# Expert sums issued in pairs, a modulation row made later, and more PSUM banks for the first norm, in a one-core decoder step

## The chip, the cores and the metric

The kernel runs on one core of a Trainium2 chip. The metric is the device time of one execution in microseconds. Everything below is from three timed runs of the kernel before and one profiled execution of it.

## The reference, cut to what matters

One decoder layer over 1088 tokens: 1024 of a prompt and 64 of a sample group (8 sequences of 8). A mixer (a gated short convolution and gated linear attention) comes first, then a PEER layer that picks, for each token and head, 16 of 16384 experts. Both are wrapped in norms with a modulation (shift, scale, gate) made from a condition.

```python
def decoder_layer(x, c, conv_buf, gla_state, params):
    mod = (jax.nn.silu(c) @ w_ada + b_ada)[:, None, :]
    sh1, sc1, g1, sh2, sc2, g2 = jnp.split(mod, N_MOD, axis=-1)
    h = rms_norm(x, n_mix_pre) * (1.0 + sc1) + sh1
    m, new_buf, new_state = mixer(h, ...)
    x = x + g1 * rms_norm(m, n_mix_post)
    h = rms_norm(x, n_ffn_pre) * (1.0 + sc2) + sh2
    x = x + g2 * rms_norm(peer(h, ...), n_ffn_post)
...
def peer(h, wq, subkeys, u_tab, v_tab):
    ...
    gate = jax.nn.softmax(top_v, axis=-1)
    act = jax.nn.gelu(jnp.einsum('thkd,td->thk', u_tab[expert], xb))
    return jnp.einsum('thk,thkd->td', gate * act, v_tab[expert])
```

## The kernel before

**Staging.** The 1088 tokens lie in nine tiles: two of the prompt (128 tokens each), the sample tile (64), six more of the prompt. Three tiles make a block (block 0: tiles 0, 1 and the sample tile). After a conditioning phase and the attention heads, each block goes through `mix_phase`, `merge_phase`, `out_phase`, `norm_phase`, `keys_phase` and `pick_phase`; `last_phase` closes the kernel. The experts that `pick_phase` chooses are fetched and used by `Gather`, which runs token by token beside the phases of the next block, and alone in the last phase. How many tokens each phase takes is fixed by `SHARES` (L2266) through `Turns`: 67, 35, 28, 30, 64 and 72 in block 1's phases, 87, 46, 35, 39, 84 and 93 in block 2's.

**Gather.** For one token the 128 chosen rows (8 heads x 16) are fetched by one indirect DMA from GpSimd (L1042): 128 rows of u and v, 2048 floats each. Ten such buffers exist (`NUV`). TensorE spreads the token's h over 128 partitions in two half spreads of 512 columns (L1059, banks 0 and 1; half spread s waits for dot s - 2). VectorE multiplies each half with u and adds up (L1164), ScalarE makes a gelu of four tokens (L1134), VectorE weighs them (L1184). TensorE then sums gate times v (L1079): each token of a group of four adds a matmul of 32 output rows per half of D, at PSUM partitions j*32 (j is the token's row group: 0 to 3 by turns in a prompt tile, 0 and 1 in the sample tile) in bank 2 or 3. All eight matmuls of a group stand in one block behind half spread 8q + 11 (`spread` and `summed`, L1046 to L1083), and `v_mm`, raised by the last one, frees the four buffers for GpSimd's next fetches. [...]

**Modulation and the first norm.** `Modulation` makes the rows GATE1, SHIFT2, GAIN2 and GATE2 (nine rows each: the prompt's and eight sequences') while block 0 is in its phases, before the gather needs `gat.uv`, whose buffers it borrows. It has eight chunks of 512 columns, at the steps `AT` (L1218): 2 MB of weights by SyncE, eight matmuls into four row groups (L1289), a copy by ScalarE (L1309), a folding matmul (L1299), two operations of VectorE on 9x512 (L1319, L1321), and a save by SyncE. Chunks 6 and 7 (GATE2) come at steps 0 and 2 of block 0's `norm_phase`; their weights are fetched in `merge_phase`. `norm_phase` needs rows spread over all partitions: `spread_row` (L1743) does it with two matmuls of K = 9 into two banks. It has banks 4 to 7 for that, so in block 0 the prompt's and the sample's GATE1 rows come first, GAIN2 takes their banks once VectorE has used them, SHIFT2 takes the banks of GAIN2. VectorE goes through squares (L1838), gate, addition of x and squares (L1843, L1847, L1850), gain (L1856), shift (L1861), each over three tiles, then TensorE transposes (L1780).

## Time and profile before

| | us |
|---|---|
| median of 3 runs | 4248.77 (4247.3 to 4263.02) |
| profiled execution | 4251.55, span 4249.7 |
| TensorE busy | 3195.1 (75%) |
| VectorE busy | 2578.3 (61%) |
| GpSimd busy | 1605.2 (38%) |
| ScalarE busy | 839.7 (20%) |
| DMA | 1348.98 MB, mean 317 GB/s |
| first gather issued | 1040.43 |

In a profile PE is TensorE's matmuls, PEld its weight loads, DVE VectorE, ACT ScalarE, POOL GpSimd, SPq SyncE's queue. [...] Averages over the whole span mix three regimes, so the numbers are to be read by stage.

### The profile page before, as it was taken

What the parts mean: (1) busy time and instruction counts of PE and PEld (TensorE: products, weight loads), DVE (VectorE), ACT (ScalarE), POOL (GpSimd) and SP (SyncE); (2) the same over time, 40 slices, a digit from 0 to 9 for tenths busy, and PEclk for the clock granted to TensorE, in tenths of its full rate; (3) what the DMA queues carried; (4) which work ended last, traced back from release to release, by engine and by line L of the source; (5) the groups of instructions that cost most, each with busy time, mean ns of one, the idle gap of its engine ahead of it and who ended that gap; (6) DMA issues with size and microseconds to landing.
All of it is one profiled execution on the core that took longest, in us unless ns stands there. A gap on an engine that the chain in (4) does not pass through costs nothing. (4 is left out here: it accounts for less than half of the span.)

```text
span 4249.7 us, 46772 instructions
## 1 busy us (share of the span) xinstructions
PE 3195.1 (75%) x15717; PEld 1732.2 (41%) x15717; DVE 2578.3 (61%) x7848; ACT 839.7 (20%) x1341; POOL 1605.2 (38%) x1354
## 2 busy tenths in 40 slices
PE   7999988885688876766788777777666666666676
PEld 5899977754265542521255353243111111111111
DVE  2553453348765656878765566678776555655554
ACT  4233323332123222111124212111101000000000
POOL 2101105423365653443355454343333333333332
PEclk9999988977699887987899898698666666666666
DMA  7011105523899999998999999999999999999998
GB/s 263 32 46 47 52 30 187 211 97 143 316 368 393 378 412 365 367 366 343 354 394 408 391 401 402 378 413 379 360 389 382 411 415 412 407 412 411 412 408 341
DMA packets 219399, 1348.98 MB, mean 317 GB/s; under 512 B 27710, under 2 KB 37246, under 8 KB 76956
## 3 DMA queue, kind: packets, MB, share of 16 engines
q0 software_dynamic: 156672, 1140.92, 66.6%
q1 hardware_dynamic: 62492, 205.06, 13.3%
q8 instruction: 131, 2.15, 0.2%
q14 instruction: 104, 0.85, 0.1%
HBM read 1317.77 MB, written 28.10 MB: 317 GB/s over the span
## 5 line engine op out<-in xcount | busy, mean ns | idle before, releaser
L1164 DVE CUSTOM_DVE_ANT_0 peer_uv<-peer_uv,all_PS 128x512 f32<-128x512 f32 x2176 | 1436.3, 685 | 1042.4 <-DMA peer_uv<-in_uv,peer_idx 520.7
L1042 POOL DMA_INDIRECT peer_uv<-in_uv,peer_idx x1088 | 1056.4, 971 | 1495.4 <-PE all_PS L1079 1176.8
L1059 PE MATMUL all_PS<-peer_hT,peer_sel 96*128 96x512 bf16 x2176 | 982.7, 467 | 845.6 <-DVE peer_halves L1164 801.1
L1059 PEld LDWEIGHTS all_PS<-peer_hT,peer_sel 96*128 96x128 bf16 x2176 | 205.3, 101 | 1659.7 <-DVE peer_halves L1164 1330.9
L1079 PE MATMUL all_PS<-peer_uv,peer_zw 128*32 128x512 f32 x4352 | 817.3, 851 | 2.2 <-DVE peer_zw L1184 2.2
L932 POOL TENSOR_TENSOR flow_w_lo<-flow_w,flow_w_hi 128x1024 fp32r<-128x1024 f32 (+1 forms) x204 | 463.7, 2278 | 566.6 <-ACT flow_w_hi L925 566.1
L1134 ACT ACTIVATE peer_ge<-peer_pre 128x4 f32<-128x4 f32 x272 | 55.9, 205 | 2092.5 <-DVE peer_pre L1170 2092.5
L1079 PEld LDWEIGHTS all_PS<-peer_uv,peer_zw 128*32 128x32 f32 x4352 | 154.1, 141 | 426.9 <-issue 424.4
L952 PE MATMUL all_PS<-mix_h_hi,flow_w_hi 128*128 128x384 f32 (+1 forms) x672 | 283.0, 421 | 35.7 <-POOL flow_w_lo L932 31.9
L925 ACT ACTIVATE flow_w_hi<-flow_w 128x1024 fp32r<-128x1024 f32 (+1 forms) x204 | 203.7, 1003 | 317.4 <-PE all_PS L954 164.9
L953 PE MATMUL all_PS<-early_h_h_low,flow_w_hi 128*128 128x384 f32 (+1 forms) x672 | 225.6, 336 | 0.0
L954 PE MATMUL all_PS<-mix_h_hi,flow_w_lo 128*128 128x384 f32 (+1 forms) x672 | 224.9, 335 | 0.0
L1164 DVE DVE_READ_ACCUMULATOR2_ANT peer_halves<- 128x1 f32 x2176 | 179.7, 83 | 0.0
L952 PE MATMUL all_PS<-turned_h_hi,flow_w_hi 128*128 128x384 f32 (+1 forms) x384 | 177.5, 462 | 1.4 <-PEq L143 1.4
L952 PEld LDWEIGHTS all_PS<-mix_h_hi,flow_w_hi 128*128 128x128 f32 x672 | 134.2, 200 | 75.0 <-issue 40.9
L182 POOL CAST stream_w_hi<-stream_heads_w 128x1024 fp32r<-128x1024 f32 x16 | 16.6, 1038 | 357.7 <-PE all_PS L617 293.3
L953 PEld LDWEIGHTS all_PS<-early_h_h_low,flow_w_hi 128*128 128x128 f32 x672 | 131.6, 196 | 7.7
L953 PE MATMUL all_PS<-turned_h_lo,flow_w_hi 128*128 128x384 f32 (+1 forms) x384 | 131.4, 342 | 0.0
L954 PE MATMUL all_PS<-turned_h_hi,flow_w_lo 128*128 128x384 f32 (+1 forms) x384 | 130.6, 340 | 0.0
L954 PEld LDWEIGHTS all_PS<-mix_h_hi,flow_w_lo 128*128 128x128 f32 x672 | 130.3, 194 | 0.0
L1659 PE MATMUL all_PS<-flow_w_hi,out_x_hi 128*128 128x256 f32 (+1 forms) x288 | 108.6, 377 | 18.5 <-DVE join_gate_low L992 15.8
L952 PEld LDWEIGHTS all_PS<-turned_h_hi,flow_w_hi 128*128 128x128 f32 x384 | 78.7, 205 | 26.3 <-issue 25.9
(310 smaller groups left out, 4763.0 us busy)
## 6 DMA issues: line engine op xcount, KB each, us to landing
flow_w<-in_w_gate_ab SPq DMA_DIRECT2D x48, 512.0 KB, 5.4
flow_w<-in_w_query SPq DMA_DIRECT2D x48, 512.0 KB, 7.0
flow_w<-in_w_conv SPq DMA_DIRECT2D x36, 512.0 KB, 4.3
peer_uv<-in_uv,peer_idx POOLq DMA_INDIRECT x1088, 10.7
cond_w<-in_w_ada SPq DMA_DIRECT2D x6, 2048.0 KB, 10.1
stream_heads_w<-in_w_heads SPq DMA_DIRECT2D x24, 512.0 KB, 4.8
peer_uv<-in_w_ada SPq DMA_DIRECT2D x6, 2048.0 KB, 8.9
flow_w<-in_w_proj_b SPq DMA_DIRECT2D x24, 512.0 KB, 5.7
```

What stands on the lines that cost most here:

```text
L182: nc.gpsimd.tensor_copy(hi, raw).then_inc(high, 1)
L925: nc.scalar.activation(self.hi[:, i % self.pairs, 0:nk], self.raw[:, i % self.raws, 0:nk], ACT.Copy).then_inc(self.high, 1)
L932: nc.gpsimd.tensor_tensor(self.lo[:, i % self.pairs, 0:nk], self.raw[:, i % self.raws, 0:nk], self.hi[:, i % self.pairs, 0:nk].bitcast(F32 ...
L952: nc.tensor.matmul(out, w_hi[:, k, :], x.hi[:, k, :], start=(k == 0), stop=False)
L953: nc.tensor.matmul(out, w_hi[:, k, :], x.lo[:, k, :], start=False, stop=False)
L954: last = nc.tensor.matmul(out, w_lo[:, k, :], x.hi[:, k, :], start=False, stop=(k == nk - 1))
L1042: self.nc.gpsimd.indirect_dma_start(out=self.uv[:, n % self.NUV, :], out_offset=None, in_=self.A["uv"], in_offset=bass.IndirectOffsetOnAxi ...
L1059: nc.tensor.matmul(PS[:, f, :], self.sel[:, m:m + 1].broadcast_to([3 * GR, P]), self.hT[:, g % self.NH, f * 512:(f + 1) * 512], start=True ...
L1079: last = nc.tensor.matmul(PS[j * GR:(j + 1) * GR, 2 + e, :], self.zw[:, z, GR - 1 - c:2 * GR - 1 - c], self.uv[:, n % self.NUV, D + e * 51 ...
L1134: nc.scalar.activation(self.ge[:, q % self.ND, :], self.pre[:, q % self.ND, :], ACT.Gelu_apprx_tanh).then_inc(M["gelled"], 1)
L1164: nc.vector.tensor_tensor_reduce(part, part, PS[:, f, :], 1.0, 0.0, ALU.mult, ALU.add, self.halves[:, d, f, e:e + 1]).then_inc(M["dotted"], 1)
L1659: nc.tensor.matmul(bank(j), x.hi[:, k, tok], w_hi, start=(k == 0), stop=False)
```

## The change

Three parts.

1. `summed` is called four times per group, for two tokens and one half of D each, behind four half spreads in a row (8q + 10 to 8q + 13) rather than twice behind 8q + 11.
2. The two chunks of GATE2 leave `Modulation`. A new class `LastGate` makes the row in block 0's `pick_phase`, in four rounds of 256 columns at steps 4, 9, 14 and 19, with buffers and semaphores of its own.
3. In block 0's `norm_phase` the row spreadings use banks 0 to 3 as well (the gather has not begun): both GAIN2 rows are spread at the start, SHIFT2's prompt row once all gates are used, SHIFT2's sample row once the prompt gains are.

```diff
-            if n >= BT and f == 1 and n % BT == 1:
-                for e in range(2):
-                    self.summed(pe, n // BT - 1, e)
+            q, p = divmod(s - 2 * BT - 2, 2 * BT)
+            if q >= 0 and p < 4:
+                self.summed(pe, q, p)
...
-    def summed(self, pe, q, e):
+    def summed(self, pe, q, p):
...
-        if e == 0:
+        e, pair = divmod(p, 2)
+        if p == 0:
             pe.wait_ge(M["weighed"], q + 1)
...
-        for n in range(BT * q, BT * q + BT):
+        for n in range(BT * q + 2 * pair, BT * q + 2 * pair + 2):
...
-        if e:
+        if p == 3:
             last.then_inc(M["v_mm"], 1)
...
-    AT = (8, 12, 17, 22, 29, 33, NORM, NORM + 2)
-    LINES = ((GATE1, 0.0), (SHIFT2, 0.0), (GAIN2, 1.0), (GATE2, 0.0))
+    AT = (8, 12, 17, 22, 29, 33)
+    LINES = ((GATE1, 0.0), (SHIFT2, 0.0), (GAIN2, 1.0))
...
+class LastGate:
+    AT = (4, 9, 14, 19)
+    WN = 256
...
+    def fetch(self, sp, s):
+        for r in self.here(s + 3):
+            half = slice(r % 2 * self.WN, (r % 2 + 1) * self.WN)
+            if r:
+                sp.wait_ge(self.used, r)
+            sp.dma_start(self.w[:], self.A["w_ada"][10 + r // 2, :, :, half]).then_inc(self.w_in, 16)
+            if r:
+                sp.wait_ge(self.lined, r)
+            for dst, src in ((self.bias, "ada_rows"), (self.gain, "gain_rows")):
+                sp.dma_start(dst[:, :], self.A[src][6 + r // 2:7 + r // 2, half].broadcast_to([NC, self.WN])).then_inc(self.small_in, 16)
...
+    def product(self, pe, s):
+        CT = P // 4
+        for r in self.here(s):
+            pe.wait_ge(self.w_in, 16 * r + 16)
+            if r:
+                pe.wait_ge(self.rowed, r)
+            for k in range(KD):
+                j = k % 4
+                last = self.nc.tensor.matmul(self.PS[j * CT:(j + 1) * CT, FRONT + 1, 0:self.WN], self.later.cols[:, k, :], self.w[:, k, :],
+                                             start=(k < 4), stop=(k >= 4), skip_group_check=True)
+            last.then_inc(self.used, 1)
+        for r in self.here(s - 1):
+            pe.wait_ge(self.rowed, r + 1)
+            if r:
+                pe.wait_ge(self.added, r)
+            self.nc.tensor.matmul(self.PS[0:NC, FRONT + 2, 0:self.WN], self.later.folds, self.row[:, :],
+                                  start=True, stop=True).then_inc(self.folded, 1)
...
+    def make_line(self, dve, s):
+        for r in self.here(s - 2):
+            dve.wait_ge(self.folded, r + 1)
+            dve.wait_ge(self.small_in, 32 * r + 32)
+            if r:
+                dve.wait_ge(self.kept, 16 * r)
+            self.nc.vector.tensor_tensor(self.line[:, :], self.PS[0:NC, FRONT + 2, 0:self.WN], self.bias[:, :], ALU.add).then_inc(self.added, 1)
+            dve.wait_ge(self.added, r + 1)
+            self.nc.vector.tensor_tensor(self.line[:, :], self.line[:, :], self.gain[:, :], ALU.mult).then_inc(self.lined, 1)
...
+        GATE_AT, GAIN_AT, SHIFT_AT = ((FRONT, FRONT + 2), (0, 2), (FRONT + 2, 0)) if part.samples else ((FRONT,), (FRONT,), (FRONT + 2,))
+        Y_AT = FRONT + 2
+        row = lambda at: PS[:, at:at + 2, :].rearrange("p b d -> p (b d)")
...
-            spread_row(GATE1, 0, False)
+            spread_row(GATE1, GATE_AT[0], False)
             if part.samples:
-                spread_row(GATE1, 1, True)
+                spread_row(GATE1, GATE_AT[1], True)
+                spread_row(GAIN2, GAIN_AT[0], False)
+                spread_row(GAIN2, GAIN_AT[1], True)
             else:
-                spread_row(GATE2, 1, False)
+                spread_row(GATE2, Y_AT, False)
...
                 if stage == 2 and i == 0:
-                    pe.wait_ge(gated, prompts)
-                    spread_row(GAIN2, 0, False)
-                    if part.samples:
-                        pe.wait_ge(gated, nt)
-                        spread_row(GAIN2, 1, True)
-                    else:
+                    pe.wait_ge(gated, nt)
+                    if not part.samples:
+                        spread_row(GAIN2, GAIN_AT[0], False)
                         pe.wait_ge(fin.done, 1)
-                        spread_row(SHIFT2, 1, False)
+                    spread_row(SHIFT2, SHIFT_AT[0], False)
                 if stage == 3:
+                    pe.wait_ge(gained, prompts)
                     if part.samples and i == 0:
-                        pe.wait_ge(gained, nt)
-                        spread_row(SHIFT2, 1, False)
-                    if i == sample:
-                        pe.wait_ge(h2_done, prompts)
-                        spread_row(SHIFT2, 1, True)
-                    pe.wait_ge(gained, prompts)
+                        spread_row(SHIFT2, SHIFT_AT[1], True)
...
             for j in range(NJ):
                 gat.turn(sp, upto(j))
+                if gate:
+                    gate.fetch(sp, j)
+                    gate.keep(sp, j)
```

The rest of `LastGate` is the copy of a product's rows by ScalarE and the save of a line by SyncE, at the next steps; `pick_phase` calls all of them by engine and step.

## Rows read from the trace of the kernel before

**Rows 1.** The page's slices of the span in tenths, 106 us each.
```profile
PEclk9999988977699887987899898698666666666666
DMA  7011105523899999998999999999999999999998
```

**Rows 2.** The chain that ended last, pieces of it: start us, us, what.
```profile
3748.11 12.78 DMA peer_uv<-in_uv,peer_idx
3762.97 3.12 PE all_PS L1079 x16
```

**Rows 3.** Table by stretch: start:end, length, busy (count) by engine, PEclk, DMA share, GB/s.
```profile
1137.00:1347.00 210.00, 189.56 (x1062) 135.14 (x1058) 122.67 (x326) 63.24 (x84) 123.45 (x92) 0.96 0.97 384
1347.00:1565.00 218.00, 169.65 (x969) 113.36 (x969) 127.97 (x328) 44.42 (x69) 119.37 (x89) 0.90 0.97 386
1660.00:1850.00 190.00, 149.61 (x828) 93.70 (x828) 138.99 (x597) 35.05 (x65) 91.72 (x75) 0.94 0.94 371
1850.00:2090.00 240.00, 159.70 (x481) 36.00 (x481) 189.30 (x700) 21.15 (x44) 78.24 (x79) 0.76 0.90 355
2090.00:2357.00 267.00, 224.67 (x1198) 142.27 (x1198) 161.25 (x431) 79.53 (x102) 147.00 (x115) 0.94 0.99 395
2357.00:2612.00 255.00, 191.81 (x1060) 117.81 (x1062) 155.74 (x404) 43.29 (x72) 129.44 (x104) 0.90 0.99 396
2728.00:2950.00 222.00, 174.90 (x930) 101.00 (x930) 162.81 (x674) 33.83 (x68) 101.03 (x88) 0.90 0.97 391
2950.00:3234.00 284.00, 181.64 (x623) 35.71 (x623) 223.15 (x813) 26.31 (x54) 97.86 (x102) 0.68 0.96 379
3234.00:4200.00 966.00, 656.36 (x2230) 122.68 (x2228) 548.66 (x1715) 60.26 (x137) 355.91 (x371) 0.66 1.01 410
```

**Rows 4.** Timeline of block 0's norm: start us, us, engine, line, operation, [idle before].
```profile
878.20 0.50 PEld L1743 LDWEIGHTS all_PS<-early_lines,early_pick 9*128 9x128 f32 x2 [3.91 <-issue]
...
885.50 0.20 PEld L1289 LDWEIGHTS all_PS<-peer_uv,peer_y 128*32 128x32 f32 x8 [1.61 <-issue]
...
891.78 0.68 DVE L1319 TENSOR_TENSOR peer_uv<-all_PS,peer_uv 9x512 f32<-9x512 f32 x1 [7.73 <-PE all_PS L1299]
...
893.10 1.26 DVE L1843 SCALAR_TENSOR_TENSOR mid_spare<-mid_spare,mid_lists,all_PS 128x1024 f32<-128x1024 f32 x1
...
913.13 2.35 DVE L1861 TENSOR_TENSOR mid_spare<-mid_spare,all_PS 128x1024 f32<-128x1024 f32 x2 [3.94 <-PE all_PS L1743]
...
914.47 0.71 PEld L1780 LDWEIGHTS all_PS<-all_ident,mid_spare 128*128 128x128 f32 x4 [3.02 <-issue]
...
922.74 1.21 DVE L1861 TENSOR_TENSOR mid_spare<-mid_spare,all_PS 64x1024 f32<-64x1024 f32 x1 [4.94 <-PE all_PS L1743]
...
927.27 0.28 PEld L952 LDWEIGHTS all_PS<-turned_h_hi,flow_w_hi 128*128 128x128 f32 x1 [1.57 <-issue]
```

**Rows 5.** Timeline, sums of a prompt group in the end stage.
```profile
3701.27 0.20 PEld L1079 LDWEIGHTS all_PS<-peer_uv,peer_zw 128*32 128x32 f32 x8 [0.44 <-issue]
...
3702.13 0.20 PEld L1079 LDWEIGHTS all_PS<-peer_uv,peer_zw 128*32 128x32 f32 x4 [0.66 <-issue]
...
3704.42 0.11 PEld L1059 LDWEIGHTS all_PS<-peer_hT,peer_sel 96*128 96x128 bf16 x2 [1.24 <-issue]
```

**Rows 6.** Timeline, sums of a prompt group in block 1's mix.
```profile
1216.44 0.16 PEld L1079 LDWEIGHTS all_PS<-peer_uv,peer_zw 128*32 128x32 f32 x8 [0.23 <-issue]
...
1216.89 0.13 PEld L1079 LDWEIGHTS all_PS<-peer_uv,peer_zw 128*32 128x32 f32 x4 [0.30 <-issue]
...
1218.29 0.19 PEld L952 LDWEIGHTS all_PS<-mix_h_hi,flow_w_hi 128*128 128x128 f32 x1 [0.84 <-issue]
```

**Rows 7.** Timeline, sums of a group of the sample tile.
```profile
1920.99 0.19 PEld L1079 LDWEIGHTS all_PS<-peer_uv,peer_zw 128*32 128x32 f32 x4 [0.44 <-issue]
...
1921.85 0.18 PEld L1079 LDWEIGHTS all_PS<-peer_uv,peer_zw 128*32 128x32 f32 x2 [0.67 <-issue]
```

**Rows 8.** The waits, whole span: who waited for whom, us, times, longest.
```profile
DVE peer_uv L1164 <- PE all_PS L1059: 508.3, 348, 6.7
```

More of the change, by code:

```diff
@@ L1250, in fetch @@
             sp.dma_start(self.folds, self.A["folds"]).then_inc(self.cols_in, 16)
-        for c in self.early(s):
+        for c in self.here(s + 4):
             e = c % 2
@@ L1311, in make_line @@
     def make_line(self, dve, s):
-        for c in self.late(s):
+        for c in self.here(s - 1):
             e = c % 2
@@ L1687, in _, with norm_phase @@
                 gat.dots(dve, turns.upto(j))
-def norm_phase(nc, A, G, part, gat, m_rows, brought, junk, work, ended, later, h, lo, hi):
+def norm_phase(nc, A, G, part, gat, m_rows, brought, junk, work, ended, h, lo, hi):
     with Phase(nc, f"norm{part.index}", G["flow"]) as sc:
@@ L1986, in lows, with pick_phase @@
         return 2 * self.tiles
-def pick_phase(nc, A, G, part, gat, best, place, ended, following, brought, lo, hi):
+def pick_phase(nc, A, G, part, gat, best, place, ended, later, following, brought, lo, hi):
     with Phase(nc, f"pick{part.index}", G["flow"]) as sc:
@@ L2045, in _ @@
                 gat.spread(pe, upto(j))
+                if gate:
+                    gate.product(pe, j)
                 if j == FIN:
@@ L2331, in hybrid_decoder @@
                             h = Turned(after, part.n, nt)
-                            norm_phase(nc, A, G, part, gat, m_rows, early, junk, work, ended[0], later, h, marks[3], marks[4])
+                            norm_phase(nc, A, G, part, gat, m_rows, early, junk, work, ended[0], h, marks[3], marks[4])
                             early.free()
@@ L2338, in hybrid_decoder @@
                             h_early = early_h(following)
-                        pick_phase(nc, A, G, part, gat, best, place, ended[1], following, h_early, marks[5], marks[6])
+                        pick_phase(nc, A, G, part, gat, best, place, ended[1], later, following, h_early, marks[5], marks[6])
                     w0, lo = w0 + len(once), marks[6]
```

65 lines of the change are left out of this document (37 added, 28 removed).

## Prediction

> **What bounds the kernel now.** I read the page's slices first, then the chain that ended last, a table by stage, and the timeline of a few places. Up to 1040 us no gather of expert rows runs, and each phase follows the one before it; whatever shortens a phase there moves all that follows. From 1040 us to the end the DMA engines are nine tenths busy or more [rows 1], and the chain is a loop: rows land, TensorE sums them, GpSimd issues the next gather, and its rows land about 12.8 us later [rows 2]. The table by stage shows how tight each stage is [rows 3]: DMA share 1.01 in the last 966 us, 0.97 to 0.99 in the mix stages of blocks 1 and 2 (1137:1347, 2090:2357), 0.90 and 0.96 in their picking stages (1850:2090, 2950:3234), which are VectorE's (189 of 240 us and 223 of 284 us busy). In the mix stages TensorE is a second bound beside the DMA: 189.6 of 210 us and 224.7 of 267 us busy. So there are three regimes: serial (norm of block 0), two bounds at once (mix, merge, out, keys of blocks 1 and 2), DMA alone (the end).
>
> **Part 1, the norm of block 0.** It runs from 878.3 to 927.3 us, 49.0 us [rows 4]. The change takes out chunks 6 and 7 of the modulation, their waits among them: VectorE waits 7.7 us for the first folded row (ahead of 891.78), and it runs four operations of 0.68 us for the two lines. It also spreads GAIN2's two rows at the start and SHIFT2's prompt row into banks that are free by then, where now each spreading waits until VectorE has used the bank. VectorE waits 3.9 us ahead of 913.13 and 4.9 us ahead of 922.74 [rows 4]. Two spreadings take 7.3 us (first weight load at 878.20, product of chunk 6 at 885.50), so 3.65 us each; four of them end at 892.8. I step through VectorE's queue with the durations of the rows (1.2 for squares and additions, from 2.35 for two at 913.13; 1.26 for scalings). Squares of three tiles end at 884.1 (891.78 less the wait of 7.7). The second stage is three times 1.26 + 1.2 + 1.2 = 11.0 us and needs only the two gate rows and the roots: it ends at 895.1 if no root is late. The gains need GAIN2's rows (889 and 892.8), the saved x2 and the last root, about 2 us behind the last square: they end near 899.3. SHIFT2's prompt row is spread from 893 to 896.5; the sample's row waits for the prompt gains (898) and ends at 901.5, and the transposes of tile 0 stand behind it on TensorE. The rest, from the first transposes to the end, is 927.3 - 914.5 = 12.8 us now, 4.9 of it the wait for the last shift row, which goes: about 8 us. End near 909.3, so the phase takes 31 us and **-18 us** come out. What is late next is TensorE with its six spreadings at 3.65 us; VectorE waits under 3 us at a time. Bounds: the phase can't fall under VectorE's own work, about 27 us (-22); if the four spreadings hold the second stage up, and each saved tile is late, 35 us (-14). The fetches of the two chunks also leave the merge stage of block 0; I cost that at nothing (0 to -2), since their 4 MB land beside weights that arrive in time.
>
> **Part 2, the second gate's chunks in block 0's picking.** Four rounds of 256 columns instead of two of 512. VectorE gets two operations on 9x256 per round; 9x512 takes 0.68 us [rows 4], so 0.35 to 0.68 each, 3 to 5 us in all, of which one round (0.8 us) lies ahead of the first gather and the rest in a stage whose VectorE is the limit. TensorE's eight products per round are half of those at 885.50; nothing urgent is queued behind them on TensorE but the next half spread, about 2 us later at most. SyncE waits for the line of round 1 before it can go on; behind it are only the row fetches of later groups. ScalarE waits for each product; behind it is a gelu of four tokens. 4 MB that ran in the merge stage now partly share the DMA engines with the first 24 tokens. **+3 us** (0 to +8).
> [...]
>
> **Part 3, the sums in pairs.** A group is four tokens; its eight matmuls (four tokens, two halves of D) each write 32 output rows at j*32 and make two records. Now they stand in one block behind half spread 8q+11. How they run together is in three places of the timeline. In prompt tiles the four tokens have j = 0, 1, 2, 3: weight loads come as 8, 4, 4 with 0.86 us between them at 1.2 GHz [rows 5] and 0.43 us at 2.4 GHz [rows 6]: four rounds of four records. In the sample tile j is only 0 and 1: loads come as 4, 2, 2, ... with 0.86 us between [rows 7], eight rounds of two. So a round is as wide as there are different j side by side. A pair of the change has two j, and a half spread, which takes all columns, stands between the pairs: two rounds per pair, **eight rounds per group instead of four** in prompt tiles, the same eight in the sample tile. To it comes the change between the two kinds of matmul: 0.23 us idle ahead of the block and 0.13 behind its last round (1218.29 - 1216.44 = 1.85 for four rounds of 0.43) [rows 6]. One pair costs 0.86 + 0.13 + 0.10 = 1.1 us (the 0.10 is what a half spread's weight load waits less for when a full-width matmul follows it), four cost 4.4, against 1.85 + 0.1 now: **+2.4 us of TensorE per prompt group at 2.4 GHz**. At 1.2 GHz it is 3.15 us now [rows 5] (its last round already faster) and 4 x 1.85 = 7.4 then: +4.
>
> What lies beside other work goes by stage [rows 3]. The kernel's shares give the groups: 17 in mix 1, 16 in merge and out 1, 16 in keys 1, 22 in mix 2, 20 in merge and out 2, 21 in keys 2. TensorE busy plus 2.4 us each:
> mix 1: 190 + 41 = 231 in a stage of 210; keys 1: 150 + 38 = 188 of 190; merge and out 1: 170 + 38 = 208 of 218; mix 2: 225 + 53 = 278 of 267; keys 2: 175 + 50 = 225 of 222; merge and out 2: 192 + 48 = 240 of 255.
> A busier TensorE also gets its full clock for more of the stage (granted 0.90 to 0.96 now), which gives back 5 to 10 us in the larger ones. I take mix 1 at +18, mix 2 at +12, keys 1 and 2 at +8 each, the two merge and out stretches at +5 each, since neither bound can be filled fully beside the other, and the norms of blocks 1 and 2 (17 groups) at +4 together: **+60**. All hidden but the excess in the mixes would be +12; with no idle time usable beyond today's, +95.
> Slots come free later too: the last pair stands behind half spread 8q+13, a token later, in exchange for a start half a token earlier. A gather takes 2.5 us of the engines (1.05 MB at 410 GB/s), and one that is issued behind two others lands 12.8 us later [rows 2], so some three are in flight when the first of four is issued. The later release eats part of these 7 us, and the engines don't run dry as long as the delay is under 4 us or so; I take none of it into the sum.
>
> Picking stages: VectorE waits for half spreads that stand behind the block; over the whole kernel 508 us in 348 waits [rows 8]. The pairs split one wait of two to three us into four of up to one, but half of the tokens of a burst now have a pair ahead of them and less of the block lies under picking work. I take **+5** for both together (-20, if the DMA idle of 0.10 x 240 us is half won back, to +30).
> The end, 93 groups: a group takes 966 x 4 / 371 gathers = 10.4 us, set by DMA. TensorE then needs, at 2.4 GHz, four half spreads with a pair at 1.3 us and four without at 0.75 us (VectorE's pace): 8.2 us; at 1.2 GHz 4 x 2.4 + 3 = 12.6. Its granted clock is 0.66 there: it rises behind the block and falls again among the lone half spreads. With the pairs it is busy for longer at a stretch, so I expect a mix of both levels, about 9.8 us, under the 10.4: **+5** (0 to +40).
> [...] The sample tile, where rounds are two wide too, has a granted clock of 0.76 in its stage [rows 3].
>
> **The sum.** -18 + 3 + 60 + 5 + 5 = +55 us, against the profiled execution's own 4251.55 us (span 4249.7); that run lies 2.8 us above the median of three, 4248.77. I predict **4303 us** as a median.
>
> **Rivals.**
> *Hidden in the DMA's shadow* (no change): the extra rounds fall in TensorE's idle time and only the two mixes' excess of some 10 to 15 us shows. For it: DMA share 0.97 to 1.01. Against it: 231 in 210. 4249 - 18 + 3 + 13 = 4247.
> *Faster*: a half spread that waits for one pair instead of a block lets VectorE and so the slots run earlier. DMA idle, one less the share times the length, is 24 + 11 us in the picking stages, 18 in the keys stages, 18 elsewhere in [rows 3]; winning back 30 of these 71 us with the pairs nearly free gives 4249 - 15 - 30 = 4204. It decides if pairs of different j overlap across the half spread; the timeline shows no record doing so.
> *Much slower*: in the end stage the clock stays at 1.2 GHz for most of the group, and TensorE takes the place of DMA: 11.5 to 12.6 us per group instead of 10.4, 93 groups: +100 to +200 us, 4400 to 4500. It decides when a group passes 10.4 us, which is when more than two of its four pairs run at the lower clock.
> *The change doesn't do what it says*: TensorE starts the next pair's loads early so that a group still takes four rounds; that is the first rival's time.
>
> **Chances.** Forecast 0.50; hidden 0.21; faster 0.15; much slower 0.14. The range 4232 to 4385 holds the forecast with the bounds of its parts and most of the hidden case, and leaves out the two outer rivals in large part. A difference under 0.5% (21 us) can't be told from none: faster by more 0.14, within 0.22, slower by more 0.64.
>
> **What would show it.** Norm of block 0 at 30 to 33 us, with no wait over 3 us on VectorE. Sums in prompt tiles: rounds of two records, eight to a group, with half spreads between. TensorE over 0.97 busy in both mixes, which take 225 us and 278 us or so, with the DMA share down to 0.92. End stage at 10.4 to 10.6 us per group, granted clock over 0.75. I am wrong in the main step if the mixes keep their length, or if the group in the end stage grows by over 0.5 us.

## The result and the profile after

| | before | changed |
|---|---|---|
| median | 4248.03 us (4 runs) | 4441.97 us (4 runs, 4439.46 to 4444.28) |
| profiled execution | 4251.55, span 4249.7 | 4443.31, span 4441.4 |
| TensorE busy | 3195.1 (75%) | 3633.3 (82%) |
| granted clock, mean | 0.807 | 0.868 |
| first gather issued | 1040.43 | 1020.35 |

The ratio of the means is 1.0448 (95% interval 1.0424 to 1.0473): 4.5% slower; by the medians 194 us, where 55 had been forecast and 4385 was the top of the range. The step in the norm came out as forecast and brings the first gather forward by 20 us; everything is lost behind it.

The page's slices of the changed kernel, to be laid beside [rows 1]:

```profile
PEclk9999989886999988987899898798777888888888
DMA  6011115437889998988889999998899999999998
```

PEclk is the granted clock of TensorE as a share of its full one, here in tenths. It is higher in the last twelve slices (7 and 8 for 6), and the DMA share is lower in seven slices from the twelfth to the 29th. What the prediction and the expectations call 2.4 GHz and 1.2 GHz shows in the traces as a granted clock of 1.00 and of 0.50 (before, 1216.40:1218.30 and 3701.27:3702.10), with 0.43 us [rows 6] and 0.86 us [rows 5] from one round's loads to the next; no run shows a frequency. The table by stretch (start:end, length, busy and count by engine, PEclk, DMA share, GB/s): mix 1, keys 1, the picking behind it, mix 2 and 966 us of the end, against [rows 3].

```profile
1129.00:1375.00 246.00, 231.91 (x1068) 135.87 (x1068) 127.32 (x331) 65.26 (x86) 126.05 (x94) 0.98 0.89 340
1707.00:1937.00 230.00, 197.45 (x864) 96.86 (x864) 157.50 (x679) 36.09 (x68) 98.64 (x80) 0.93 0.89 340
1937.00:2161.00 224.00, 157.25 (x447) 26.61 (x445) 171.66 (x616) 20.36 (x41) 70.62 (x73) 0.77 0.88 342
2161.00:2453.00 292.00, 272.34 (x1200) 142.09 (x1199) 164.40 (x433) 79.70 (x102) 150.73 (x116) 0.97 0.94 368
3405.00:4371.00 966.00, 741.23 (x2179) 124.03 (x2180) 548.99 (x1679) 59.75 (x135) 349.83 (x362) 0.82 1.00 400
```

With nearly the same count of TensorE's records (1068 for 1062, 1200 for 1198), mix 1 takes 246 us for 210 and mix 2 takes 292 for 267. TensorE is busy for 232 of 246 and 272 of 292 us (231 and 278 had been worked out): 0.94 and 0.93, where over 0.97 was forecast. The DMA share has gone from 0.97 to 0.89 and from 0.99 to 0.94: neither bound is met. In the end stage 362 gathers are issued in 966 us where it was 371. Who waits is in the view of VectorE's waits of the changed kernel (us in total, times, longest), against 508.3 in 348 times for TensorE before [rows 8]. The third line is the wait for rows before:

```profile
DVE peer_uv L1164 <- PE all_PS L1058: 820.6, 760, 7.7
DVE peer_uv L1164 <- DMA peer_uv<-in_uv,peer_idx: 357.3, 295, 8.4
...
DVE peer_uv L1164 <- DMA peer_uv<-in_uv,peer_idx: 520.7, 418, 6.0
```

VectorE's dots wait 312 us longer for the half spreads, in twice as many places, and 163 us less for rows.

**Where the time went.** For each run below I cut the span at the issue of the gather four tokens ahead of each phase's first token, from the rows of the timeline. "gather" is the issue of the first gather, "start" that of token 28 (tokens counted from 0); then come the lengths of the six phases of block 1, the six of block 2, the end, and the span, all in us of the profiled execution. The labels are those of the experiments.

```
             gather start  mix  merge  out  norm  keys  pick  mix  merge  out  norm  keys  pick   end  span
before         1040  1132  218    125   91    94   214   216  268    149  109   115   247   258  1016  4250
changed        1020  1124  251    133  102    97   231   224  292    160  117   124   271   281  1036  4441
no_pairs       1019  1115  219    123   93    93   211   216  268    149  111   116   247   258  1017  4235
pairs_only     1038  1137  250    133   99    97   225   227  293    163  117   127   273   282  1035  4459
narrow         1017  1112  219    120   96    94   214   216  271    149  110   117   250   258  1018  4244
late           1018  1114  223    125   92    90   217   235  271    152  110   117   257   259  1038  4300
early          1026  1127  221    122   90   103   211   237  267    149  112   123   260   272  1017  4311
halves         1020  1119  222    123   90    99   210   227  268    153  109   119   256   265  1016  4277
two_two        1023  1130  246    127   94   106   227   229  284    158  115   131   274   295  1022  4436
barrier        1025  1127  248    130   91   106   227   229  283    153  119   133   264   294  1082  4485
dummy          1026  1129  253    133   98   108   236   221  295    159  120   142   274   303  1128  4600
dummy_split    1026  1123  258    126   91    97   217   216  295    153  116   118   262   264  1013  4348
odd_wide       1019  1112  223    123   92    89   210   214  266    149  109   113   251   254  1017  4222
mid_wide       1016  1115  223    125   94    95   217   227  267    153  109   119   256   262  1019  4282
odd_two        1015  1111  241    125   93    94   219   217  281    152  114   120   260   266  1030  4323
even_two       1012  1119  245    132   99   107   228   228  281    156  113   129   279   288  1016  4419
```

The changed kernel loses in every stage behind the 28th token: 33 and 24 us in the mixes, 17 and 24 in the keys, 8 and 23 in the picking stages, 20 at the end.

The first column is also a measure of scatter. From `no_pairs` on, all kernels but `pairs_only` run the same instructions up to the first gather, yet it is issued between 1012 us (`even_two`) and 1026 us (`dummy_split`). There is one profile for each kernel, so up to 14 us of "start" can't be laid to an edit; differences of 2 or 3 us in a stage can't either (`narrow` against `no_pairs`).

### The profile page after: what moved, and what is told of

It is laid out like the page before. It is cut to its first block and busy times, and to the rows that moved or that the text cites. A ratio compares the mean times of both kernels' runs of the same rounds, so it can differ in the third digit from the quotient of the medians.

```text
span 4441.4 us, 46871 instructions
## 1 busy us (share of the span) xinstructions
PE 3633.3 (82%) x15753; PEld 1729.2 (39%) x15753; DVE 2601.3 (59%) x7852; ACT 839.7 (19%) x1343; POOL 1616.0 (36%) x1354
## 5 line engine op out<-in xcount | busy, mean ns | idle before, releaser
L1164 DVE CUSTOM_DVE_ANT_0 peer_uv<-peer_uv,all_PS 128x512 f32<-128x512 f32 x2176 | 1462.4, 685 | 1221.1 <-PE all_PS L1058 820.6
L1041 POOL DMA_INDIRECT peer_uv<-in_uv,peer_idx x1088 | 1069.0, 983 | 1837.3 <-PE all_PS L1079 1545.3
L1058 PE MATMUL all_PS<-peer_hT,peer_sel 96*128 96x512 bf16 x2176 | 915.8, 432 | 604.5 <-DVE peer_halves L1164 556.6
L1079 PE MATMUL all_PS<-peer_uv,peer_zw 128*32 128x512 f32 x4352 | 1378.1, 718 | 13.4 <-DVE peer_zw L1184 13.4
L951 PE MATMUL all_PS<-mix_h_hi,flow_w_hi 128*128 128x384 f32 (+1 forms) x672 | 269.5, 401 | 36.9 <-POOL flow_w_lo L931 31.8
L1079 PEld LDWEIGHTS all_PS<-peer_uv,peer_zw 128*32 128x32 f32 x4352 | 170.6, 117 | 327.9 <-issue 295.3
L951 PE MATMUL all_PS<-turned_h_hi,flow_w_hi 128*128 128x384 f32 (+1 forms) x384 | 165.4, 431 | 1.4 <-PEq L143 1.4
L1727 PE MATMUL all_PS<-flow_w_hi,out_x_hi 128*128 128x256 f32 (+1 forms) x288 | 102.6, 356 | 11.5 <-DVE join_gate_low L991 8.7
```

Of the source, the lines that this page charges most:

```text
L951: nc.tensor.matmul(out, w_hi[:, k, :], x.hi[:, k, :], start=(k == 0), stop=False)
L1041: self.nc.gpsimd.indirect_dma_start(out=self.uv[:, n % self.NUV, :], out_offset=None, in_=self.A["uv"], in_offset=bass.IndirectOffsetOnAxi ...
L1058: nc.tensor.matmul(PS[:, f, :], self.sel[:, m:m + 1].broadcast_to([3 * GR, P]), self.hT[:, g % self.NH, f * 512:(f + 1) * 512], start=True ...
L1079: last = nc.tensor.matmul(PS[j * GR:(j + 1) * GR, 2 + e, :], self.zw[:, z, GR - 1 - c:2 * GR - 1 - c], self.uv[:, n % self.NUV, D + e * 51 ...
L1164: nc.vector.tensor_tensor_reduce(part, part, PS[:, f, :], 1.0, 0.0, ALU.mult, ALU.add, self.halves[:, d, f, e:e + 1]).then_inc(M["dotted"], 1)
L1727: nc.tensor.matmul(bank(j), x.hi[:, k, tok], w_hi, start=(k == 0), stop=False)
```

## Experiments

**Which part.** `no_pairs` is the changed kernel with `summed` as before, `pairs_only` the kernel before with the pairs alone. The first diff is against the changed kernel, those that follow are against `no_pairs`; all are cut to what matters.

```diff
-            q, p = divmod(s - 2 * BT - 2, 2 * BT)
-            if q >= 0 and p < 4:
-                self.summed(pe, q, p)
+            if n >= BT and f == 1 and n % BT == 1:
+                for e in range(2):
+                    self.summed(pe, n // BT - 1, e)
```

> The changed kernel with the sums put back as one block behind half spread 8q+11. Theory (the pairs carry the whole loss, the two other parts give 15 to 20 us): 4228 to 4234 us. Rival (the gate's row in block 0's picking costs as much as the norm gives, since from the first gather to the 28th the changed kernel took 103.5 us against 91.5): 4243 to 4250.

Measured 4238.54 us, ratio 0.9978 (0.9966 to 0.9990): a gain of 9 us by the ratio, 15 by the profiled spans, and a median between the two forecasts.

> The kernel before with the sums in pairs alone. Both theories of the loss (rounds half as wide, slots released later) expect 4248 + 205 to 215 = 4453 to 4463. Rival (the loss comes from the pairs together with the gate's row): under 4430.

Measured 4451.68, ratio 1.0477 (1.0454 to 1.0500), some 203 us. The pairs carry the whole loss and the two other parts a small gain; there is no interaction worth its name.

**Is it the width of the rounds?** `narrow` leaves the block where it was and only changes the order in it.

```diff
-        for n in range(BT * q, BT * q + BT):
+        for e in range(2):
+            for n in range(BT * q + 2 * pair, BT * q + 2 * pair + 2):
```

> As no_pairs, the eight sums of a group in one block behind 8q+11, but in the order tokens 0 and 1 (both halves of D), then tokens 2 and 3, so that only two row groups lie side by side: eight rounds of two records in one place. It has the extra TensorE time of the pairs (about 1.7 us a group at 2.4 GHz) and releases the slots only by that much later. Theory TensorE (the extra rounds are the cost): 4380 to 4430. Theory release (the loss is what the later release costs, 3 us in the changed kernel, and this has 1.7 of them): about 0.57 x 205 = +117, 4345. Neither (the cost is the switching between half spreads and pairs): 4240 to 4280.

Measured 4242.44 (0.9982, 0.9967 to 0.9998): no different from `no_pairs`. The number lies in the range of the third reading (4240 to 4280), but it decides nothing between the three, since the edit didn't do what I made it for. The timeline of its mix 1 (start, us, engine, line, operation) shows weight loads of 8, 4 and 4 as in [rows 6], 16 for the eight products, and phase work 1.87 us behind the first of them:

```profile
1214.77 0.17 PEld L1079 LDWEIGHTS all_PS<-peer_uv,peer_zw 128*32 128x32 f32 x8 [0.23 <-issue]
1215.23 0.14 PEld L1079 LDWEIGHTS all_PS<-peer_uv,peer_zw 128*32 128x32 f32 x4 [0.29 <-issue]
1215.65 0.14 PEld L1079 LDWEIGHTS all_PS<-peer_uv,peer_zw 128*32 128x32 f32 x4 [0.29 <-issue]
1216.64 0.19 PEld L951 LDWEIGHTS all_PS<-mix_h_hi,flow_w_hi 128*128 128x128 f32 x1 [0.84 <-issue]
```

In this block the order of the eight products made no difference; in both orders tried, products of four row groups run side by side. If only what takes all columns parts them, one full-width product will. So `barrier` puts one tiny full-width product of zeros between the pairs (left out in the first column of a tile):

```diff
+        if pair and c:
+            nc.tensor.matmul(PS[:, 2, 0:1], self.G["ident"][:, :], self.zw[:, BT * q % (self.NZ * BT), GR:GR + 1],
+                             start=False, stop=False, skip_group_check=True)
```

> The run narrow with one product of zeros over all 128 output rows and one column between tokens 0, 1 and tokens 2, 3, which must part the two pairs' rounds: eight rounds of two in one block behind 8q+11, 3.4 us instead of 1.7 at 2.4 GHz. It is the rounds' time alone, in one piece, with a release later by that time only. Theory (TensorE's time): 4238 + 1.7 to 3.4 us for each of some 250 groups outside DMA's shadow; by the run dummy (366 us for 2.6 to 5.2 us a group) in proportion +230 to 240, 4470. Rival (in that run it was the one long block, beyond the 1.5 us that VectorE has to do, that cost): also above 4400; under 4330 it would mean that rounds cost little and the places carry the loss.

Measured 4488.75 (1.0570, 1.0533 to 1.0608), +250 over `no_pairs`. Both readings had it above 4400, so the total doesn't tell the rounds' time from the length of the one piece. Its timeline in mix 1: loads of 4, 2, 2, the full-width product at 1225.57, loads of 4, 2, 2 again (left out), and phase work 4.00 us behind the first.

```profile
1223.73 0.14 PEld L1082 LDWEIGHTS all_PS<-peer_uv,peer_zw 128*32 128x32 f32 x4 [0.23 <-issue]
1224.19 0.12 PEld L1082 LDWEIGHTS all_PS<-peer_uv,peer_zw 128*32 128x32 f32 x2 [0.31 <-issue]
1224.62 0.12 PEld L1082 LDWEIGHTS all_PS<-peer_uv,peer_zw 128*32 128x32 f32 x2 [0.31 <-issue]
1225.57 0.30 PEld L1076 LDWEIGHTS all_PS<-peer_zw,all_ident 128*128 128x128 f32 x2 [0.84 <-issue]
...
1227.73 0.19 PEld L951 LDWEIGHTS all_PS<-mix_h_hi,flow_w_hi 128*128 128x128 f32 x1 [0.84 <-issue]
```

`narrow` also bears on the order in which products start. Were it strictly that of the program, tokens 2 and 3 could start in `narrow` only beside the second halves of tokens 0 and 1, two rounds later, which makes six rounds, 2.6 us by an estimate from 0.43 us a round; it took 1.87. That speaks against a strict order in this block.

**Is it the time on TensorE?** `dummy` adds three products with weights of zero behind the block, after the release; `dummy_split` lays them, one each, behind three second half spreads.

```diff
+            if j == 3 and c < GR - 1:
+                for k in range(3):
+                    nc.tensor.matmul(PS[0:GR - 1, 2, :].rearrange("p (a b) -> p a b", a=4), self.zw[:, z, GR:2 * GR - 1],
+                                     self.G["ident"][:, :].unsqueeze(1).to_broadcast([P, 4, P]),
+                                     start=False, stop=False, skip_group_check=True)
```

> no_pairs with extra TensorE work behind the release: after the block of each prompt group (but a tile's last) three products with weights of zero are added into row group 0, six rounds of one record, 6 x 0.43 = 2.6 us at 2.4 GHz; no slot is released later by it. It prices TensorE's time alone. Theory (in the stages of blocks 1 and 2 TensorE's time is the cost, the later release costs in the sample tile's stage and at the end): the changed kernel's loss less that of the run late, 205 - 66 = +135, so about 4374, the mixes 25 us longer each and the end as in no_pairs. Rival (TensorE's time is hidden unless the release is late too): under 4290.

> The run dummy with its three products of zeros laid behind 8q+11, 8q+13 and 8q+15, one each (0.86 us at 2.4 GHz), rather than all behind the block: the same TensorE time in short pieces at the ends of tokens. If TensorE's total time sets the loss, as in dummy: 4570 to 4610. If the length of one uninterrupted piece does (VectorE has two half spreads, 1.5 us of work, to bridge it): 4350 to 4450.

Measured 4604.06 (1.0855, 1.0832 to 1.0878) and 4348.14 (1.0235, 1.0202 to 1.0268): +366 and +110 for the same six extra rounds in a group. `dummy` lies far above both of its forecasts, `dummy_split` 2 us under the lower of its own. So a sum of TensorE's work can't price this change. Short pieces behind a token cost mostly where TensorE is full: by the table 39 and 27 us in the mixes, 6 and 15 in the keys, 13 more up to the end of block 1 (7 of them ahead of the first gather, where the kernels are the same) and 17 over the rest of block 2, and the end is not longer. In one piece they cost 112 us in the end alone.

**Is it the late release?** `late` moves the whole block behind 8q+13, `early` behind 8q+10.

```diff
-            if n >= BT and f == 1 and n % BT == 1:
+            if n >= BT + 2 and f == 1 and n % BT == 2:
```

> As no_pairs, the block with its four rounds of four, but behind half spread 8q+13, where the last pair of the changed kernel stands: a later release by one token, no more TensorE time. Theory TensorE: within 15 us of no_pairs, 4230 to 4250. Theory release: nearly the whole loss, 4380 to 4430.

Measured 4304.37 (1.0140, 1.0114 to 1.0167): +66, of it 19 in the sample tile's picking stage, 6 and 10 in the keys and 21 at the end. Neither theory holds.

```diff
-            if n >= BT and f == 1 and n % BT == 1:
+            if n >= BT and f == 0 and n % BT == 1:
```

> no_pairs with the whole block half a token earlier, behind 8q+10. If the place of the release sets the end stage (late is 23 us longer there for one token later), this gives back up to 10 us there: 4220 to 4235. If the block then waits on TensorE for the weights of its last token, the stages with phase work lose: 4245 to 4270.

Measured 4312.70 (1.0170, 1.0148 to 1.0193). Slots come free earlier and it is slower by 74 us, beyond both readings: 12 up to the 28th token (7 of them ahead of the first gather, and so not the edit's), 10 in norm 1, 21 and 14 in the picking stages, 13 in keys 2, and nothing in the mixes or at the end. Those are stages whose phase work lies on VectorE and is laid between whole tokens.

`halves` and `two_two` cut it in two parts behind 8q+10 and 8q+11, the one by halves of D, the other by tokens:

```diff
-            if n >= BT and f == 1 and n % BT == 1:
-                for e in range(2):
-                    self.summed(pe, n // BT - 1, e)
+            q, e = divmod(s - 2 * BT - 2, 2 * BT)
+            if q >= 0 and e < 2:
+                self.summed(pe, q, e)
```

> no_pairs with the four tokens' products of one half of D behind 8q+10 and those of the other behind 8q+11: it cuts the block in two as the change wants, but keeps rounds of four records and the place of the release. Theory: +0.3 us of TensorE a group for one more switch, and a release at most 0.5 us earlier: 4230 to 4245. If cutting by itself costs, 4260 or more.

Measured 4277.16 (1.0088, 1.0061 to 1.0114): half the block in that place costs about half of it. The forecast of 4230 to 4245 missed; the cut by itself is not the cost, as `odd_wide` below shows.

> no_pairs with a group's sums in two parts: tokens 0 and 1 in both halves of D behind 8q+10, tokens 2 and 3 behind 8q+11. Each part is four rounds of two records, eight to a group as with the pairs, but all behind the half spread of before: the release is later by under 1 us. Theory (TensorE's time): + 2.2 us of TensorE a group, 4340 to 4380, the end within 8 us of no_pairs. Rival (the release must be late for a loss): under 4270.

Measured 4432.16 (1.0443, 1.0416 to 1.0470), above the forecast of either reading and nearly the changed kernel, with the end within 5 us of `no_pairs`, as expected.

**Place and width, two by two.** What `early` points to is the place of a piece: behind the first half spread of a token (8q+10, 8q+12) or behind its second (8q+11, 8q+13). Four runs cut the block in two parts. In the wide ones a part is four tokens' products of one half of D (rounds of four), in the `two` ones two tokens' products of both (rounds of two). The diff is that of the odd ones; `mid_wide` and `even_two` have `s - 2 * BT - 2`.

```diff
+            q, p = divmod(s - 2 * BT - 3, 2 * BT)
+            if q >= 0 and p in (0, 2):
+                self.summed(pe, q, p // 2)
```

> no_pairs with the four tokens' products of one half of D behind 8q+10 and the other half's behind 8q+12: rounds of four, but both parts stand between the first and the second half spread of a token, as two of the four pairs do, and the release is later by half a token. Theory (a part inside a token holds up VectorE's second dot, and with it the phase's work that stands behind the token; the run early lost 74 us that way, in the norm, picking and second keys stages, halves lost 39): 4300 to 4330. Rival (only rounds and the late release count): 4238 + about 30 = 4260 to 4275.

> no_pairs with tokens 0 and 1 (both halves of D) behind 8q+11 and tokens 2 and 3 behind 8q+13: eight rounds of two and the changed kernel's late release, but both parts behind a token's second half spread. If the rounds' time on TensorE is the main cost: 4390 to 4440, near the changed kernel. If the places inside a token carry half of it: 4330 to 4370.

> odd_two with both parts half a token earlier: tokens 0 and 1 behind 8q+10, tokens 2 and 3 behind 8q+12, each four rounds of two records, now between a token's first and second half spread. TensorE's work and its cut are those of odd_two (4337), the release is half a token earlier. Theory (a piece inside a token costs by its length, since VectorE has one dot and none of the phase's work to bridge it): 4420 to 4470. Rival (four pieces in a row make the rest of the changed kernel's loss, not the place): 4310 to 4340.

> late cut in two: the four tokens' products of one half of D behind 8q+11, those of the other behind 8q+13, rounds of four, both at the ends of tokens, the release as late as in late and odd_two. Theory (late release alone, the switch hidden): within 15 us of late, 4290 to 4315, and 25 to 45 under odd_two, which is then the price of the rounds at the ends of tokens. Rival (odd_two's loss over no_pairs is all rounds and none of it the late release): 4240 to 4260.

| medians, us (ratio to before) | behind second half spreads | behind first half spreads |
|---|---|---|
| rounds of four | odd_wide 4228.31 (0.9959, 0.9944 to 0.9974) | mid_wide 4284.27 (1.0083, 1.0058 to 1.0108) |
| rounds of two | odd_two 4337.15 (1.0213, 1.0179 to 1.0246) | even_two 4421.64 (1.0416, 1.0387 to 1.0445) |

The width costs 109 us at the ends of tokens, the place 56 with rounds of four; together they cost 193, so 28 come from both at once: a piece inside a token costs by its length. `even_two` came out at the lower end of its theory's range, `mid_wide` between its two forecasts. `odd_two` fell between the two forecasts made for it (4330 to 4370 and 4390 to 4440), inside the lower one, which stood for the place carrying half. `odd_wide` fell on the rival's side, 12 us under its range: with the release as late in the program as in `late`, nothing is lost. It has the lowest median of the study, but its interval touches that of `no_pairs` (0.9966 to 0.9990). `late` therefore did not price the late release alone, as I had taken it.

How the place works is in two timelines of the second picking stage, both at a granted clock of 0.50 in the part's first round (0.86 us from one round's loads to the next). TensorE's products and the accumulator's reads are left out. First `even_two` (start, us, engine, line, operation, [idle before <- releaser]):

```profile
3195.42 0.19 PEld L1079 LDWEIGHTS all_PS<-peer_uv,peer_zw 128*32 128x32 f32 x4 [0.44 <-issue]
3195.64 0.69 DVE L1164 CUSTOM_DVE_ANT_0 peer_uv<-peer_uv,all_PS 128x512 f32<-128x512 f32 x1
...
3198.85 0.11 PEld L1058 LDWEIGHTS all_PS<-peer_hT,peer_sel 96*128 96x128 bf16 x2 [1.54 <-issue]
3199.28 0.69 DVE L1164 CUSTOM_DVE_ANT_0 peer_uv<-peer_uv,all_PS 128x512 f32<-128x512 f32 x1 [2.95 <-PE all_PS L1058]
...
3199.90 1.22 DVE L2198 TENSOR_TENSOR pick_eq<-pick_twice,pick_digits 128x2048 bf16<-128x2048 bf16 x1
```

VectorE does one dot, waits 2.95 us for the token's second half spread, which stands behind the part, and only then comes to the 1.22 us of picking that needed nothing from TensorE. Then `odd_two`:

```profile
3105.52 0.19 PEld L1079 LDWEIGHTS all_PS<-peer_uv,peer_zw 128*32 128x32 f32 x4 [0.44 <-issue]
3105.67 0.68 DVE L1164 CUSTOM_DVE_ANT_0 peer_uv<-peer_uv,all_PS 128x512 f32<-128x512 f32 x1
3106.28 1.22 DVE L2198 TENSOR_TENSOR pick_eq<-pick_twice,pick_digits 128x2048 bf16<-128x2048 bf16 x1
...
3107.53 1.23 DVE L2202 TENSOR_TENSOR pick_eq<-pick_eq,pick_places 128x2048 bf16<-128x2048 bf16 x1
3108.79 1.58 DVE L2204 TENSOR_TENSOR pick_eq<-pick_eq 128x1024 bf16<-128x1024 bf16 x3
3109.08 0.13 PEld L1058 LDWEIGHTS all_PS<-peer_hT,peer_sel 96*128 96x128 bf16 x2 [1.66 <-issue]
```

The same part, 3.56 us from its first load to the next half spread, lies under the picking work, and VectorE doesn't wait. Picking work is the first shelter of a token's start. The second is the wait for the token's rows. Summed over the rows of the timelines (us, the dots' waits for PE ahead of the first and of the second half, and for DMA, which all stand ahead of the first):

```
             PE, 1st   PE, 2nd   DMA    sum    median
odd_wide       242        41     712     995   4228
no_pairs       515        44     449    1008   4239
before         465        44     521    1030   4248
halves         346       279     401    1026   4277
mid_wide        85       435     554    1074   4284
late           425        40     613    1078   4304
early           94       596     386    1076   4313
odd_two        641        43     424    1108   4337
dummy_split    735        46     335    1116   4348
even_two        97       808     275    1180   4422
two_two        442       570     174    1186   4432
changed        407       413     357    1177   4442
barrier       1098        51     112    1261   4489
dummy         1218        59      54    1331   4604
```

The sum follows the time, but for inversions of up to 9 us between neighbours. Inside a token a wait for TensorE comes on top; ahead of one, part of it is time in which the rows would not have been there anyway. `barrier` and `dummy` show the limit of that shelter: nearly all of their waits for TensorE are ahead of tokens, and the waits for rows, at 112 and 54 us, have little left to give.

## Why the prediction was wrong, point by point

**Norm of block 0: right.** 31 us were forecast. The first spreading starts at 874.24 and the keys at 906.12, 31.9 us for 49.0 [rows 4]. The timeline of the changed kernel:

```profile
874.24 0.29 PEld L1809 LDWEIGHTS all_PS<-early_lines,early_pick 9*128 9x128 f32 x2 [3.02 <-issue]
...
889.58 0.49 PEld L1809 LDWEIGHTS all_PS<-early_lines,early_pick 9*128 9x128 f32 x2 [4.20 <-DVE mid_spare L1898]
...
895.65 2.35 DVE L1916 TENSOR_TENSOR mid_spare<-mid_spare,all_PS 128x1024 f32<-128x1024 f32 x2
...
906.12 0.29 PEld L951 LDWEIGHTS all_PS<-turned_h_hi,flow_w_hi 128*128 128x128 f32 x1 [1.57 <-issue]
```

The shifts at 895.65 follow with no wait, where 3.9 us stood before. The phase also starts 4 us earlier than before, where I had allowed 0 to 2 for the fetches that leave the merge stage; no run parts their absence from scatter, since kernels that are the same up to there start this phase anywhere between 866.8 us (`even_two`) and 880.8 us (`dummy_split`). The length of the phase is steady: 31.2 to 32.0 us in all of them.

**The gate's row in the picking: right.** From the first gather to the 28th token's, `no_pairs` takes 95.4 us (1019.08 to 1114.52) for 91.5 before: +4, where +3 was forecast. The net of both parts, 15 us by the spans and 9 by the ratio, is under the 17 that stand at the 28th token.

**Eight rounds instead of four: right in kind, too small in size.** In mix 1 of the changed kernel, half spreads without and with a pair between them, and behind them two of `no_pairs` with the whole block between them:

```profile
1215.41 0.10 PEld L1058 LDWEIGHTS all_PS<-peer_hT,peer_sel 96*128 96x128 bf16 x1 [0.16 <-DVE peer_halves L1164]
...
1216.70 0.10 PEld L1058 LDWEIGHTS all_PS<-peer_hT,peer_sel 96*128 96x128 bf16 x1 [0.16 <-issue]
...
1217.99 0.10 PEld L1058 LDWEIGHTS all_PS<-peer_hT,peer_sel 96*128 96x128 bf16 x1 [0.16 <-issue]
1218.31 0.14 PEld L1079 LDWEIGHTS all_PS<-peer_uv,peer_zw 128*32 128x32 f32 x4 [0.23 <-issue]
1219.29 0.19 PEld L951 LDWEIGHTS all_PS<-mix_h_hi,flow_w_hi 128*128 128x128 f32 x1 [0.84 <-issue]
...
1220.45 0.10 PEld L1058 LDWEIGHTS all_PS<-peer_hT,peer_sel 96*128 96x128 bf16 x1 [0.16 <-issue]
```

```profile
1216.93 0.10 PEld L1058 LDWEIGHTS all_PS<-peer_hT,peer_sel 96*128 96x128 bf16 x1 [0.16 <-issue]
1217.25 0.16 PEld L1078 LDWEIGHTS all_PS<-peer_uv,peer_zw 128*32 128x32 f32 x8 [0.23 <-issue]
...
1220.27 0.10 PEld L1058 LDWEIGHTS all_PS<-peer_hT,peer_sel 96*128 96x128 bf16 x1 [0.16 <-issue]
```

Half spreads follow each other in 2.46 us with a pair and in 1.29 without (1215.41 to 1216.70), so a pair costs 1.17; 1.1 was taken, with a term of 0.10 for a half spread's weight load that was the author's estimate and that no run shows by itself. With the block behind them, two half spreads of `no_pairs` lie 3.34 us apart (1216.93 to 1220.27), 2.05 more than without: 4 x 1.17 - 2.05 = 2.6 us of TensorE a group, where 2.4 was forecast. The rounds' price in the clean case, `odd_two` less `odd_wide`, is 18 and 15 us in the mixes (forecast 18 and 12), 9 and 9 in the keys (8 and 8), 3 and 8 in merge and out (5 and 5), 12 in the two norms (4), 15 in the picking stages and 13 at the end (5 and 5): 101 us in the profiled spans (109 by the medians), against +70 forecast for these terms. The two kernels differ by the four extra rounds alone, 1.7 us a group; the 2.4 us of the forecast had two more switches in it. That a busier TensorE is granted more of its clock, which was to give back 5 to 10 us in the larger stages, was an estimate too: from before to the changed kernel the clock went from 0.96 to 0.98 in mix 1 and from 0.94 to 0.97 in mix 2, but from 0.94 to 0.93 in keys 1, where TensorE went from 150 of 190 to 197 of 230 us busy. The mixes and keys are close; the norms, the picking stages and the end are what makes 101 of 70. The largest miss of the sum is not here.

**The step that failed: the picking stages' and the other stages' waits.** The prediction said that "the pairs split one wait of two to three us into four of up to one" and that less of the block lies under picking work, and took +5. It counted where TensorE's time falls and not between which two of VectorE's instructions. Two of the four pairs stand behind a first half spread, where VectorE has one dot of 0.69 us to bridge them; in the block before, it had two dots and the phase's work. The changed kernel's dots wait 413 us ahead of second halves, where it was 44.

What the place alone costs is `even_two` less `odd_two`, with the same rounds and the same cut: 84 us by the medians, 96 by the spans. By stage that is 33 us in the picking stages, 28 in the keys, 22 in the norms, 16 in merge and out, 4 in the mixes and 8 up to the 28th token, while the end is 14 shorter. `even_two` comes to within 20 us of the changed kernel (4422 of 4442), and from the first gather to the end stage the changed kernel is 6 us the shorter of the two: width and place together are the loss up to there. By stage they differ more: the changed kernel is 6 and 11 us longer in the mixes, and 10, 5, 8 and 7 us shorter in the two norms, keys 2 and picking 2. In mix 1 half spreads stand 2.46 us apart with a pair between them and 3.33 us with a part of `even_two` (medians), 1.29 without either, so four pieces take 0.6 us more of TensorE in a group than two, which would lengthen the mixes; shorter pieces inside tokens would shorten the other stages. Both reasons are argued, not shown.

**The end stage.** +5 was forecast with 0 to +40 as its range, and it is +20. The group period came out just above what was said (966 x 4 / 362 = 10.67 us where 10.4 to 10.6 was given), the clock as said (0.82 where over 0.75 was). The rival in which the clock stays low and TensorE takes DMA's place did not come. The granted clock was 0.66 with TensorE busy for 656 of 966 us before, and 0.82 with 741 of 966 in the changed kernel. Busy time alone doesn't set it: over the end stage it was 0.88 with 794 of 1013 us busy in `dummy_split` and 0.79 with 896 of 1128 in `dummy`. What is left is the release, which I had put at nothing "as long as the delay is under 4 us or so". From the end of the dots of token 4q+4 to the next gather the timelines have, at the end, 4.3 us before, 4.4 in `no_pairs`, 5.4 in `odd_wide`, 5.7 in `even_two`, 6.5 in `odd_two` and in the changed kernel, 6.9 in `late`; the end stage takes 1016, 1017, 1017, 1016, 1030, 1036 and 1038 us. So in these runs 1.4 us of delay are free and 2.2 or more cost 14 to 21 us. It is an ordering, not a proof: the length of a piece costs at the end by itself, as `dummy` shows with a release at 4.3 us and 1128 us, and `barrier` takes 1082 us with 6.4 us. No run moves the release alone.

**The total.** The forecast's terms came to +55 against the profiled run; the spans differ by +192, the medians by +194. From one kernel to the next, by the medians and in brackets by the spans: -20 (-27) from the kernel before to `odd_wide`, +109 (+101) from there to `odd_two`, the rounds, where +70 was taken; +84 (+96) to `even_two`, the place, where nothing was (the +5 of the picking stages is counted in the 70); and +20 (+23) to the changed kernel, nearly all at the end, where nothing was taken for the release. The profiled execution of `odd_two` lies 12 us under its median, which is why the two ways part there. Of the first term -15 by the spans are the two other parts, just as forecast (`no_pairs`); the rest is the place of the block in `odd_wide`. The rounds are 31 to 39 above forecast, and the place is what took the time out of the range: without it 4442 would be under 4385.

The range failed in one term, the upper bound of +95 for the pairs in the mixes, merge, out, keys and norms "with no idle time usable beyond today's". Its working isn't given and it doesn't follow: the 112 groups outside the norms, at 2.4 us each, would be 269 us. Against `no_pairs` these stages lost 56 + 36 + 44 + 12 = 148 us. The forecast counted how much of TensorE's added work fits into its idle time in a stage. `dummy` and `dummy_split` show that the same added work costs 366 or 110 us by how it is cut, and `even_two` against `odd_two` that it costs 84 more by its place: VectorE stands still, and the loop of slots with it, while TensorE has idle time elsewhere in the stage. The rival *much slower* gave 4400 to 4500 and so held the time, but by luck: its reason was a low clock and 11.5 us or more for a group at the end, and neither came.

## What to carry to other kernels

Where one engine's queue feeds two customers, the place of a long piece counts beside its length (84 and 56 us here for half a token): put it where the engine that waits has its largest stock of other work queued, behind the last feed of a unit and not between its halves. Small products that share the array should stand together whenever a full-width one would part them (eight rounds a group for four cost 109 us here, `odd_two` less `odd_wide`). Here that gives `odd_wide`: the block cut by halves of D, rounds of four, behind 8q+11 and 8q+13, with the two other parts of the change: 4228 us, 0.9959 of the kernel before; whether it beats `no_pairs` (0.9978) isn't settled by these runs.

## What the runs showed of the hardware

- TensorE overlaps products of different row groups in both orders tried: 1.85 us for a group in one [rows 6], 1.87 in the other (`narrow`). One full-width product of a single column between them makes it 4.00.
- The end stage, where the DMA share was 0.99 in `no_pairs`, took six more short rounds in a group for nothing: with `dummy_split` it is 1013 us for 1017 (one profile each), while its granted clock rises from 0.65 to 0.88. In one piece behind the block the same rounds made it 1128 us, at 0.79.
- The time up to the first gather scatters by 14 us between kernels whose instructions up to there are the same; one profile each doesn't tell whether that goes by kernel or by execution.
